# Streaming encoder step with 32 experts on one core: the last stage by tiles beside the last four experts, folding in each expert

## What is computed

```python
hn = rmsnorm(h, norm_ffn)                     # h: residual after the mixer
h = h + hier_moe(hn)                          # below
y = rmsnorm(h, norm_final)                    # y_sample, y_prompt (meta rows dropped)

def hier_moe(x):                              # 32 experts in 4 groups of 8
    g = argmax(softmax(x @ w_rg + b_rg))      # one group
    top_v, top_i = top_k(softmax(logits of the group's 8 experts), 2)
    gates = p_g * top_v / sum(top_v)
    ...
    for each token t and each of its two experts e:
        out[t] += gate * ((silu(x[t] @ w_eg[e]) * (x[t] @ w_eu[e])) @ w_ed[e])
```

## Time and profile before

| what | us |
|---|---|
| median of 3 runs | 1104.85 (1103.49 to 1107.43) |
| the profiled execution | 1103.76 |
| its span, first to last instruction | 1101.9 |
| tiles and routing | 0 to 509.6 |
| 32 experts | 509.6 to 1052.9 |
| last stage | 1052.9 to 1101.9 |
| TensorE, VectorE, ScalarE, GpSimd busy | 1012.4, 417.4, 240.8, 104.8 |

### The profile page before, as it was taken

The page is one execution under the profiler, slowest core; times in us unless marked ns, Lnnn a source line. Parts: engine busy times, 40 slices in busy tenths (PEclk is TensorE's granted clock), DMA queues, the critical chain, the costliest instruction groups (busy, mean ns, idle before and its releaser), DMA issues.

```text
span 1101.9 us, 32850 instructions
## 1 busy us (share of the span) xinstructions
PE 1012.4 (92%) x14634; PEld 822.7 (75%) x14634; DVE 417.4 (38%) x909; ACT 240.8 (22%) x506; POOL 104.8 (10%) x172
## 2 busy tenths in 40 slices
PE   5999999999999999875999999999999999999920
PEld 5786777768685958435888898898888888988910
DVE  1434443535253535243432332332322323323338
ACT  2352232323332321210111111011111111111123
POOL 0110101010110101001111011011110110110000
PEclk9999999999999999986999999999999999999965
DMA  8900000000000000384999999999999999999557
GB/s 272 402 5 39 1 39 0 38 0 38 4 34 38 0 38 1 152 322 173 373 375 393 405 399 411 408 404 401 398 410 403 395 409 404 397 405 401 215 214 300
DMA packets 50850, 262.17 MB, mean 238 GB/s; under 512 B 8205, under 2 KB 10701, under 8 KB 42618
## 3 DMA queue, kind: packets, MB, share of 16 engines
q1 hardware_dynamic: 41050, 234.05, 53.8%
q0 software_dynamic: 7168, 18.10, 4.8%
q10 hardware_dynamic: 2592, 9.44, 2.1%
HBM read 241.84 MB, written 26.80 MB: 244 GB/s over the span
## 4 chain that ended last, share of the span: by engine, by line
PE 91%; DVE 5%; DMA 2%; issue 1%; ACT 1%; SPq 0%; ACTq 0%; DVEq 0%; POOLq 0%; POOL 0%
PE bank L1412 31%; PE bank L1178 18%; PE bank L1303 11%; PE bank L1423 10%; PE bank L1230 6%; PE bank L1429 5%; PE bank L1166 4%; DVE arena L1144 1%; DVE arena L1142 1%; PE bank L1279 1%; DMA arena<-in_w_in 1%; DVE arena L1150 1%; PE bank L1237 1%; PE bank L1296 1%; PE bank L1290 1%
## 5 line engine op out<-in xcount | busy, mean ns | idle before, releaser
L1178 PE MATMUL bank<-xnT,arena 128*128 128x128 f32 x1728 | 201.5, 278 | 4.9 <-DMA arena<-in_w_in 3.5
L1178 PEld LDWEIGHTS bank<-xnT,arena 128*128 128x128 f32 x1728 | 197.1, 193 | 7.6 <-DMA arena<-in_w_in 4.0
L1412 PEld LDWEIGHTS bank<-xnT,arena 128*64 128x64 f32 x4096 | 171.8, 138 | 8.9 <-issue 8.9
L1412 PE MATMUL bank<-xnT,arena 128*64 128x96 f32 x4096 | 175.0, 248 | 2.2 <-issue 2.2
L1412 PEld LDWEIGHTS bank<-hnT,arena 128*64 128x64 f32 x4096 | 169.6, 137 | 7.4 <-issue 7.4
L1412 PE MATMUL bank<-hnT,arena 128*64 128x96 f32 x4096 | 172.8, 246 | 0.6 <-issue 0.6
L1026 DVE TENSOR_SCALAR mixT<-mixT 128x384 f32<-128x384 f32 x32 | 11.5, 360 | 324.0 <-ACT mixT L692 324.0
L1303 PE MATMUL bank<-arena,mixT 128*128 128x512 f32 x288 | 127.8, 602 | 3.0 <-DVE mixT L859 3.0
L1303 PEld LDWEIGHTS bank<-arena,mixT 128*128 128x128 f32 x288 | 54.9, 193 | 69.4 <-issue 65.7
L1423 PE MATMUL bank<-arena,silu_r 128*32 128x384 f32 x768 | 86.0, 487 | 0.5 <-issue 0.5
L1429 PE MATMUL bank<-arena,silu_r 128*32 128x256 f32 x384 | 85.9, 380 | 0.0
(11 more groups left out here) (193 smaller groups left out, 934.8 us busy)
## 6 DMA issues: line engine op xcount, KB each, us to landing
arena<-in_w_eg SPq DMA_DIRECT2D x32, 2048.0 KB
arena<-in_w_eu SPq DMA_DIRECT2D x32, 2048.0 KB
arena<-in_w_ed SPq DMA_DIRECT2D x32, 2048.0 KB, 15.4
hn_rows<-hs ACTq DMA_DIRECT2D x18, 512.0 KB, 3.5
arena<-pick_rows SPq DMA_DIRECT2D x16, 512.0 KB, 10.1
arena<-in_w_in SPq DMA_DIRECT2D x3, 2048.0 KB, 14.5
arena<-in_w_out SPq DMA_DIRECT2D x1, 4096.0 KB, 25.7
out_y_prompt<-arena SPq DMA_DIRECT2D x8, 512.0 KB, 3.5
```

Source lines behind the costliest of these rows:

```text
L1178: last = mm(out, w_in_sb[:, k, a:b], xnT[:, k, :], start=k == 0, stop=k == KD - 1)
L1412: last = mm(out[q * SW:(q + 1) * SW, n * BLOCK:(n + 1) * BLOCK], w[:, k, m * P + q * SW:m * P + (q + 1) * SW], rowsT[b][:, k, :], start=k ...
```

## The change

What moves:

- **Experts weight their own rows.** The rank matmul now carries four values for each pick and not one (`VALS`: the row, the pick's gate, half of the RMS of h, the other expert of the token). For each expert ScalarE makes h_half = row times half of the RMS (`expert_half`), which is half of the residual, and VectorE makes ye = ye * gate + h_half (`fold`). The two picks of a token then add up to the final sum, and no residual or gate is needed behind them.
- **The last four experts put out their own tokens.** For experts 28 to 31 GpSimd fetches the token's other row (`fetch_other`), VectorE adds (`slot_sum`), ScalarE takes the mean square (`slot_rms`), VectorE norms (`slot_norm`) and GpSimd scatters the rows straight into the outputs. Picks whose other expert comes later are left to that one by an index out of bounds.
- **The other tokens go by tiles beside these experts.** `load_tile`, `tile_sum`, `tile_rms`, `tile_norm`, `put_tile`: one addition and one norm for each tile. pick_rows now has two halves of 2304 rows; what experts 28 to 31 write goes to the first, what a tile reads is the second.
- **Zero fill.** A tile reads rows that nobody may have written, so one DMA of SP fills all 4608 rows with zeros from hs, which GpSimd has set to zero. ScalarE waits for it (`zeros_stored`) in the first back_h, which overwrites hs.
- **Waits.** The gather of e waits for half(e-2) too; the scatter waits for the fold.

The diff's core (the index arithmetic in `places`, the extra passes and the reworked end of the ranking are cut):

```diff
+            sp.wait_ge(s["setup_pool"], 4)
+            flat_hs = hs[:, :, :].rearrange("p k n -> p (k n)")
+            sp.dma_start(y_all.rearrange("(r p) n -> p r n", p=P), flat_hs.unsqueeze(1).to_broadcast([P, 2 * PICK_ROWS // P, D])).then_inc(s["zeros_stored"], 16)
...
+            for b in range(2):
+                sp.wait_ge(ye_stored[b], 16 * (FIRST_LATE // 2))
+            load_tile(0)
+            load_late(NE - 2, "u")
+            load_tile(1)
+            load_late(NE - 2, "d")
+            load_late(NE - 1, "g")
+            load_late(NE - 1, "u")
+            sp.wait_ge(s["t_rstd"], 1)
+            load_tile(2)
+            load_late(NE - 1, "d")
+            sp.wait_ge(s["pe_g"], NE - 1)
+            load_tile(3)
+            load_tile(4)
...
+            def fetch_rows(t, b):
+                wait_parted(pool, s["pe_eT"], 2 * t + b - 1, s["parted"])
+                wait_parted(pool, s["half_ready"], 2 * t + b - 1, s["parted"])
+                gather(t, b)
...
+            def fetch_other(e):
+                pool.wait_ge(ye_stored[(e - 1) % 2], 16 * ((e - 1) // 2 + 1))
+                if e >= FIRST_LATE + 2:
+                    pool.wait_ge(s["t_out0" if e == FIRST_LATE + 2 else "t_out1"], 16)
...
+            scatter(t + 1, 1)
+            put_prompt(30)
+            put_sample(30)
+            put_tile(5)
+            put_prompt(31)
+            put_sample(31)
+            put_tile(6)
+            put_tile(7)
+            put_tile(8)
...
             def back_h(j, first=False):
                 act.wait_ge(s["h_added"], j + 1)
+                if first:
+                    act.wait_ge(s["zeros_stored"], 16)
...
+            def expert_half(t, b, first=False):
+                e = 2 * t + b
+                act.wait_ge(s["now_ready"], e + 1)
+                act.wait_ge(rows_in[b], 16 * t + 16)
+                if not (first and b == 0):
+                    act.wait_ge(s["folded"], e)
+                A(natural(h_half), turned(rows[b]), ACT.Copy, scale=now_w[b][:, 1:2]).then_inc(s["half_ready"], 1)
...
+            expert_sig(t + 1, 0)
+            expert_half(t + 1, 0)
+            tile_rms(2)
+            expert_out(t + 1, 0)
+            slot_rms(29)
+
+            expert_sig(t + 1, 1)
+            expert_half(t + 1, 1)
+            tile_rms(3)
+            tile_rms(4)
+            slot_rms(30)
+            expert_out(t + 1, 1)
...
+            def fold(t, b):
                 e = 2 * t + b
+                dve.wait_ge(s["ye_ready"], YE_STEPS * (e + 1))
+                dve.wait_ge(s["half_ready"], e + 1)
+                V.scalar_tensor_tensor(out=ye[b], in0=ye[b], scalar=now_w[b][:, 0:1], in1=h_half,
+                                       op0=ALU.mult, op1=ALU.add).then_inc(s["folded"], 1)
...
+            expert(t + 1, 0, begin=lambda: tile_norm(1))
+            slot_norm(28)
+            tile_sum(2)
+            slot_sum(29)
+            tile_norm(2)
+
+            expert(t + 1, 1, last=True)
+            tile_sum(3)
```

496 lines of the change are left out of this document (401 added, 95 removed).

## The result

| | before | after |
|---|---|---|
| median of the timed runs, us | 1104.75 (1103.49 to 1107.43) | 1120.47 (1117.51 to 1123.03) |
| profiled execution | 1103.76 | 1123.03 |
| its span | 1101.9 | 1121.1 |

The ratio is 1.0138, with a 95% interval of 1.0107 to 1.0170: the changed kernel is **slower by 1.4%**. The forecast was 1095, range 1086 to 1104. The sign is wrong, and the range did not hold the time.

The account below looks back on a forecast made before the run. The prediction took TensorE as the bound (91% of the chain), followed by a 49.0 us serial tail. It summed +12.8 front, -0.3 routing, 0 experts and -21.2 last stage to -8.7, from 1103.76 to 1095 us, range 1086 to 1104.

Parts of the forecast that it names:

- Part 1: Front: ScalarE waits for the zero fill, ending near 102.5, and TensorE's clock drops behind the gap: +12.8 us, bounds +9 to +16.
- Rival D: Front: the zero fill runs below 340 GB/s and eats up the tail's gain; at 250 GB/s 1124 us; chance 0.10.
- Part 2: Routing: added VectorE instructions hide behind other work, and the first rows are put out earlier: -0.3 us.
- Part 3: Each expert: fold, half and the later gather fit beside TensorE: cost 0; on the path up to 42 us.
- Rival E: Experts' steady beat breaks, or tile loads come after all experts; beat of 17.1 us gives 1104; chance 0.05.
- Part 4: Last stage beside experts 28 to 31: end at 1080.7 against 1101.9, -21.2 us, bounds -27.6 to -14.
- tile 1 lands at 1020, tile 2 at 1040.2: Last stage: landing times of tile rows in SP's queue, 18 us deep, counted from bytes ahead at 403 GB/s.
- No stall: Expert 30: VectorE's tile and slot work ends at 1025.7, just as its first step there is due at 1025.6.
- B: Rival: tile rows come sooner, nothing stalls beside the experts: tail -27.6, total 1088.7, or 1085 with cheaper front; chance 0.20.
- GpSimd beside VectorE: Tail: if two-SBUF-input VectorE instructions and GpSimd transfers exclude each other, end at 1085.4, sum 1099.8; given little chance.
- 3.4 us to landing: End of kernel: the last put takes 0.9 us before GpSimd's instruction, then 3.4 us to landing, ending at 1080.7.
- C: Rival: GpSimd or a deeper queue bounds the tail, -14, with front 12.8 to 16: 1098 to 1105; chance 0.19.

Follow-up runs that it names:

- e1: Changed kernel with the zero fill reading M_val, a tile nobody needs early, instead of hs: 1105.73 us, ratio 1.0030 to the kernel before.
- e2: Changed kernel with GpSimd's gather of rows also waiting for both halves of the running expert's up product: 1118.89 us, ratio 1.0147 to the kernel before.
- e3: Kernel before, with only its gather issued as late as in the changed kernel: 1103.71 us, ratio 1.0005.
- e5: Changed kernel run a second time without any edit: 1118.39 us, ratio 1.0135 to the kernel before.
- e12: Changed kernel without the early loads of tiles 0, 1 and 2, whose outputs are then not computed: 1107.20 us, ratio 1.0033 to the kernel before.
- e15: Changed kernel with tiles 0 and 1 each loaded by one transfer of 256 rows instead of two: 1114.93 us, ratio 1.0113 to the kernel before.
- e6: Changed kernel with all tile work behind the last expert's hidden values, tiles 0 and 1 still loaded early, tile 2 after the weights: 1128.24 us, ratio 1.0212.
- e7: Changed kernel with final-norm weights in PSUM for norms of tiles 3 to 8 and slots 30 and 31, each norm in halves: 1114.37 us, ratio 1.0081.
- e8: Changed kernel with tiles stored by plain transfers on ScalarE's queue and GpSimd's output stores, including the slots', left out: 1109.02 us, ratio 1.0038.
- e16: Changed kernel with fill apart, weights first, untied fetch targets, sums of tiles 2, 4, 6, 8 on TensorE, one transfer per tile: 1094.37 us, ratio 0.9915.

## Why the prediction was wrong, step by step

**Part 1, the fill: right.** +12.8 forecast. In the traces the first expert comes 11.3 and 12.5 us later, in two executions, and e1 takes 11.6 us off. The fill landed at 101.3 where 102.5 was forecast, and the clock fell as after the other gap. Rival D's mechanism, a fill below 340 GB/s, did not occur.

**Part 2, routing: right**, as far as it can be seen: -0.3 was within what front and noise leave.

**Part 3, fold and half: right.** Cost 0; the beat is 16.84. The late gather costs nothing (e2, e3). Rival E, a broken beat, occurred in the first profile for 6.4 us, in one execution, and the timed runs of e5 have their loss without it.

**Part 4, wrong, and this is the whole error**: the tail from expert 28 on was to become 21.2 us shorter, and it became 1.3 longer. 22.5 us are missing: 10.9 ahead of TensorE's end (17.8 lost where 6.9 were forecast) and 11.6 behind it (32.5 where 20.9 were forecast). From expert 28 to TensorE's end it took 67.1 us before and 84.9 changed, 68.9 without the early loads (e12), 79.1 with one transfer for each tile (e15) and 78.9 with the tiles' sums behind the hidden values (e6). So the early loads cost 16 of the 17.8 us, and either remedy alone gave back some 6.

- *The term "tile 1 lands at 1020, tile 2 at 1040.2".* Counted from expert 28's start that is 34.2 and 54.4 us; tile 0 stood 7.8 us (wu and tile 1's own bytes) ahead, at 26.4. In e15, where the rate is the old one, tile 0 lands at 34.3, tile 1 at 42.6 and tile 2 at 62.1, 7.7 to 8.4 us late each. In the changed kernel it is 40.1, 48.6 and 68.0, another 6. So two things make up the 14 us. One is the depth: the tile is issued at 14.0 and takes 20.3 us, where my sum left it 12.4. I had taken wu of 30 to land "today at 1015.7" and set tile 1 behind that, but the wait for the scatters stands ahead of wu in SP's queue and it goes out 4.4 us later; and the 18.1 us of wd, which a load took that joined this queue, gave way to a count of the bytes between two transfers. The other is the rate: the tiles' short transfers slowed the queue to 231 and 255 GB/s, where the earlier trace rows was taken to hold for any mixture, and made the weights of expert 30 late as well (20.4 us for expert 29).
- *"No stall" at expert 30.* The sum of tile 1 stands ahead of expert 30's hidden values in VectorE's order, so its landing, 14 us late, became a stall of 11.6 us there. I had written that there was "no stall, but no room"; a step with no room and a landing known to 10 us was the place for a rival, and B only went the other way.
- *GpSimd beside VectorE.* The exclusion was priced (each transfer up to 2.2 us, end at 1085.4), and given little chance because no row bore it out. No row spoke against it either: the only scatter of the trace that I looked at had VectorE idle beside it. e7 (-6.0) and e8 (-10.7) show it. From the last norm to the last issue it was 4.9 us where I had 0.9, and e7 leaves 1.7 of them. The last norm itself came 2.8 us late, in e7 as well; in e8 it came as forecast, so this part hangs on GpSimd's stores as a whole, which stand ahead of the fetch for expert 31. One transfer was stretched to 4.42 us by several VectorE instructions in a row, where I had allowed for one. The Trainium skill (SBUF — State Buffer, section Who interferes with whom) had said that such instructions contend; here the trace agrees, and the remedy that follows from it, an operand in PSUM, gave 6.0 us.
- *"3.4 us to landing" as the end.* This was read from a scatter of the kernel before, where SP ends last. Now GpSimd ends last, and from its last issue to the end of the span it takes 8.2 us. The 4.8 us were in no term and no rival, and e16 still has them (8.3).

The rivals: C named two of the mechanisms (GpSimd, a deeper queue), but its price stopped at -14 for the tail. With both at work at once, a queue deeper by 14 us and 11.6 us behind TensorE, the tail's gain is gone, and the fill at the front is left as a net cost. B (no stall) was wrong in sign. The range ended at 1104 because I let each bound stand alone, and never summed the bad ends of queue and GpSimd. With the tail as measured the sum is 12.8 - 0.3 + 1.3, which gives 1117.6, within 0.3% of both sets of runs: parts 1 to 3 hold.

What the tail shows for the idea: the same plan without the four costs (the wait for the fill, transfers by halves, tiles' sums ahead of the hidden values, and some of VectorE's sums and norms with both operands in SBUF beside GpSimd) gives 1094.37. That this is near the forecast's 1095 is chance: it is another kernel. Of the 24 us between it and the changed kernel, the first alone was measured at 11.6 and the second alone at 2.4, not clear of noise; moving the sums behind the hidden values was worse alone (e6), and its worth in the combination, with the fetches' targets freed, was not measured apart.

## What to carry to other kernels

A small load that joins a saturated queue takes the whole depth of that queue (here 20 to 26 us), and everything behind it in an in-order engine waits too: put the work that needs it behind what the bound engine waits for, and give it a target that nobody holds. The first alone, with the targets still held, lost 8.5 us (e6). Before moving work under a bound, price the *sum* of the mechanisms that could each eat a part of the gain, and look for a row in which the two engines that will now run together really do so. A fill or a clear should read from a tile that nobody overwrites early, so that the wait for it stands late, as in e1, which gained 11.6 us by one changed source.

## What the runs showed of the hardware that I had not expected

- Transfers of 0.25 and 0.5 MB in rows of 4 KB among weight loads of 2 MB, in one queue, lowered what all 16 DMA engines move from 392 to 231 to 256 GB/s for 14 us, with the engines busy throughout (1.03). The same rows by transfers of 256 rows left 391, and transfers of 0.5 MB alone went at 382.
- SP's issue of a transfer took up to 10.58 us behind the tiles' loads where it takes 0.33 otherwise, and twelve tile loads took 31.5 us to issue (with three waits of the program among them).
- GpSimd's issue of an indirect transfer took 0.91 to 1.14 us alone, and up to 4.42, 5.52 and 7.04 us beside VectorE instructions with two operands in SBUF.
- Where GpSimd issued the last transfers, the span ended 7.3 to 7.5 us behind the end of its last issue and 4.2 to 5.3 us behind the last data, with every engine idle.
- TensorE's sum of two tiles of 128x1024 by the identity took 3.4 us, against 1.23 for VectorE's.
- One profiled execution held a beat 2% longer for 24 experts, which no other profile shows.
